# A two-block transformer step in one launch: memory products interleaved with the queries, two more norms made by halves

## The reference, cut

```python
def first_block(x, mem, ...):
    h = x
    h = h + hybrid_mixer(rmsnorm(h, mix_norm), w_in, ..., w_out_mix)
    h = h + memory_cross_attention(rmsnorm(h, xattn_norm), rmsnorm(mem, mem_norm), w_q, w_kv, w_o)
    h = h + swiglu(rmsnorm(h, ffn_norm), w_gate_up, w_down)
    return rmsnorm(h, final_norm)

def memory_cross_attention(q_in, m_in, w_q, w_kv, w_o):      # q_in 1024 x 1024, m_in 256 x 1024
    q = (q_in @ w_q).reshape(bsz, s, 4, 256)
    k, v = jnp.split(m_in @ w_kv, 2, axis=-1)                # each 256 x 1024, 4 heads of 256
    scores = jnp.einsum("bshd,bmhd->bhsm", q, k)
    probs = jax.nn.softmax(scores * (256 ** -0.5), axis=-1)
    o = jnp.einsum("bhsm,bmhd->bshd", probs, v).reshape(bsz, s, D_MODEL)
    return o @ w_o

def second_block(x, c, norm_w, ada_w, ada_b, ...):
    for layer in range(2):                                   # layer 0 even, layer 1 odd
        shift, scale, gate = jnp.split(c_act @ ada_w[layer] + ada_b[layer], 3, axis=-1)
        h = rms_norm(x, norm_w[layer]) * (1.0 + scale) + shift
        y = even_mixer(h, ...) if layer % 2 == 0 else odd_mixer(h, ...)
        x = x + gate * y
    return rms_norm(x, final_norm)
```

## Time and profile before

| | us |
|---|---|
| median of 3 executions | 3113.6 (3110.55 to 3115.39) |
| the profiled execution, its own time | 3115.71 |
| its span in the trace | 3113.9 |
| PE busy | 2950.3 (95%) |
| DVE busy | 1698.2 (55%) |
| ACT busy | 1254.4 (40%) |
| mean granted clock of TensorE | 0.975 of full |

### The profile page before, as it was taken

One profiled execution on the slowest core, in us unless ns is written; L12 is line 12 of the kernel. 1 busy time (PEld: TensorE's weight loads), 2 busy tenths in 40 slices (PEclk: granted clock), 3 DMA queues, 4 the chain that ended last, 5 costly groups with the idle time before them and its releaser, 6 DMA issues. The chain is left out here.

```text
span 3113.9 us, 38755 instructions
## 1 busy us (share of the span) xinstructions
PE 2950.3 (95%) x15570; PEld 2476.2 (80%) x15570; DVE 1698.2 (55%) x2128; ACT 1254.4 (40%) x2079; POOL 385.8 (12%) x224
## 2 busy tenths in 40 slices
PE   8999998899999999999999999889999889999997
PEld 6877886788988777888888777788888768879985
DVE  6553567654454434444444735688888634316663
ACT  5321446322443111111111335577767624427751
POOL 0000006000000000000000000355445200004410
PEclk9999999999999999999999999999999989999998
DMA  4112234022202223332231212100001321131031
GB/s 147 48 43 81 94 104 181 21 61 75 75 28 68 69 85 86 86 95 72 83 95 43 98 55 65 51 1 11 11 15 35 109 95 41 54 92 44 17 111 65
DMA packets 229280, 210.99 MB, mean 68 GB/s; under 512 B 9072, under 2 KB 202864, under 8 KB 227568
## 3 DMA queue, kind: packets, MB, share of 16 engines
q1 hardware_dynamic: 225504, 195.88, 20.6%
q10 hardware_dynamic: 3600, 12.65, 1.1%
HBM read 175.93 MB, written 30.47 MB: 66 GB/s over the span
## 5 line engine op out<-in xcount | busy, mean ns | idle before, releaser
L256 DVE TENSOR_TENSOR wl<-wf,wh 128x1024 fp32r<-128x1024 f32 (+4 forms) x239 | 251.7, 1053 | 971.8 <-ACT wh L248 971.5
L248 ACT ACTIVATE wh<-wf 128x1024 fp32r<-128x1024 f32 (+4 forms) x239 | 219.9, 921 | 1130.2 <-PE P L331 994.4
L331 PE MATMUL P<-AQ,wh 128*128 128x512 f32 x1856 | 498.8, 391 | 2.5 <-issue 2.5
L2582 POOL TENSOR_TENSOR T<-T,WST 128x1024 f32<-128x1024 f32 x128 | 242.5, 1894 | 1642.5 <-DVE WST L2554 1642.5
L331 PE MATMUL P<-XH,wh 128*128 128x512 f32 (+2 forms) x1280 | 401.0, 395 | 10.8 <-DVE XL L1334 5.2
L331 PEld LDWEIGHTS P<-AQ,wh 128*128 128x128 f32 x1856 | 348.5, 188 | 76.3 <-issue 4.1
L331 PE MATMUL P<-XL,wh 128*128 128x512 f32 (+2 forms) x1280 | 397.2, 392 | 0.0
L331 PE MATMUL P<-XH,wl 128*128 128x512 f32 (+2 forms) x1280 | 396.6, 391 | 0.0
L331 PEld LDWEIGHTS P<-XH,wh 128*128 128x128 f32 (+2 forms) x1280 | 238.8, 187 | 68.5 <-issue 16.8
L331 PE MATMUL P<-AQ,wl 128*128 128x512 f32 x928 | 286.5, 390 | 0.0
L331 PEld LDWEIGHTS P<-XH,wl 128*128 128x128 f32 (+2 forms) x1280 | 239.7, 187 | 53.3
(11 more groups left out here) (418 smaller groups left out, 5150.8 us busy)
## 6 DMA issues: line engine op xcount, KB each, us to landing
AW<-ada_w SPq DMA_DIRECT2D x48, 512.0 KB, 3.7
wf<-w_gate_up SPq DMA_DIRECT2D x44, 512.0 KB, 4.9
wf<-w_in SPq DMA_DIRECT2D x28, 512.0 KB, 3.9
scratch_h<-H SPq DMA_DIRECT2D x24, 512.0 KB, 5.7
H<-scratch_h SPq DMA_DIRECT2D x24, 512.0 KB, 7.2
scratch_g<-T ACTq DMA_DIRECT2D x22, 512.0 KB, 3.0
wf<-odd_w_in SPq DMA_DIRECT2D x20, 512.0 KB, 3.8
wf<-even_w_in SPq DMA_DIRECT2D x17, 512.0 KB, 3.9
```

Source lines behind the costliest of these rows:

```text
L248: e.activation(self.sb["wh"][i % 2][:, 0:m], self.sb["wf"][i % 2][:, 0:m], ACT.Copy).then_inc(*self.s.w_hi.up(i))
L256: e.tensor_tensor(l, f, h.bitcast(F32), ALU.subtract).then_inc(*self.s.w_lo.up(i))
L331: ins = e.matmul(self.P[slot][0:m, t:t1], w, x[:, k, t:t1], start=first and k == 0, stop=last and k == kb - 1)
L2582: e.tensor_tensor(self.px(n), self.px(n), r, ALU.mult).then_inc(*s.pool.up(("sc", n)))
```

## The change

It has four parts.

**Memory.** The slabs of the memory stage come in another order, written out in a new list MEMORY: query tiles alternate with pairs of key or value slabs. The values are made in another way (`pe_memory_values`): a slab is now 256 rows of w_kv by 512 columns, and a matmul moves 512 of these columns over 128 memory rows; four slabs add up to 512 value columns in P3, 12 matmuls each. ACT and DVE empty them in two groups: group 0 goes to a staging buffer VF first, its low part stands behind slab xv 1 2, and group 1's low part stands behind the first maximum in `dve_xattn`. Queries 0 and 1 use two T buffers. The memory's split into MM comes ahead of the stage, its reload waits only for `so`; MM and KT now lie where H lies, so that H goes to scratch in eight DMAs from ACT's queue in the `so` stage, and comes back by eight DMAs on SP's queue, four behind the last value slab, four behind the scores, ahead of the third slab of the next layer; `dve_xattn_out` waits for them. `pe_xattn` waits for queries and keys head by head, and for the values of each group.

**Norm ng.** The first half's roots stand one step later (k=4), the last two tiles' residual sums and squares are in another order, and the split of slab lq0 comes behind the first half's sum instead of behind tile 6.

**Norm n5.** eo's tile 7, the norm, the inputs x5 and the pair vo are made by halves: roots of half 0 inside k=2 of the tile's second half, its spread inside k=5; roots and spread of half 1 inside the pair.

**Norm n6.** oo's tile 7 and y are made by halves; y reads the root from P3 instead of T, in 16 DVE instructions of 512 columns, and 16 output DMAs of 256 KB follow.

```diff
+MEMORY = [("q", 0), ("q", 1), ("xk", 0), ("xk", 1), ("q", 2), ("xk", 2), ("xk", 3), ("q", 3), ("xk", 4), ("xk", 5),
+          ("q", 4), ("xv", 0, 0), ("xv", 0, 1), ("q", 5), ("xv", 0, 2), ("xv", 0, 3), ("xk", 6), ("q", 6), ("xv", 1, 0),
+          ("xv", 1, 1), ("xk", 7), ("q", 7), ("xv", 1, 2), ("xv", 1, 3)]
...
-        self.slabs("q", run(dr["w_q"], 0, 8))
-        self.slabs("xk", run(dr["w_kv"], 0, 8))
-        self.slabs("xv", run(dr["w_kv"], 1024, 8), whole=True)
+        for stage in MEMORY:
+            kind, j = stage[0:2]
+            if kind == "xv":
+                c, i = 1024 + 512 * j, stage[2]
+                self.slab(stage, cols(dr["w_kv"], c, c + 512, (2 * i, 2 * i + 2)), stage)
+            else:
...
                 e.wait_ge(*self.s.dve.to(("h1", i)))
+                e.dma_start(self.dr["hT"][:, i, :], self.H[:, i, :]).then_inc(*self.s.m[i // 4].up("out" if i % 4 == 3 else None))
...
-        e.wait_ge(*self.s.mm.to(("n2", "spread")))
-        e.wait_ge(*self.s.me.to("out"))
-        e.dma_start(self.sb["MF"][:, :], self.dr["mT"].rearrange("p k t -> p (k t)")).then_inc(*self.s.me.up("back"))
+        s = self.s
+        e.wait_ge(*s.mm.to(("so", 7)))
+        e.wait_ge(*s.me.to("out"))
+        e.dma_start(self.sb["MF"][:, :], self.dr["mT"].rearrange("p k t -> p (k t)")).then_inc(*s.me.up("back"))
+        self.sp_weights(e, self.no["wo", 0] + 2)
+        for j in range(8):
+            if j % 4 == 0:
+                e.wait_ge(*s.mm.to(("xs", 15) if j else ("xv", 1, 3)))
+            e.dma_start(self.H[:, j, :], self.dr["hT"][:, j, :]).then_inc(*s.h[j].up("memory"))
         self.sp_weights(e, self.no[("gu", 0), 0] + 2)
...
+        _, c, i = stage
+        n = self.no[stage]
+        wh, wl = self.halves(n)
+        e.wait_ge(*self.s.w_hi.to(n))
+        e.wait_ge(*self.s.w_lo.to(n))
+        if i == 0:
+            self.pe_place(e, 3)
+        for b in range(2):
+            ts = slice(128 * b, 128 * b + 128)
+            for k in range(2):
+                mh, ml = self.sb["MMH"][:, 2 * i + k, ts], self.sb["MML"][:, 2 * i + k, ts]
+                ins = self.three(e, self.P[3][:, 512 * b:512 * b + 512], mh, ml, wh[:, k, :], wl[:, k, :],
+                                 i + k == 0, (i, k) == (3, 1))
+        ins.then_inc(*self.s.mm.up(stage))
+        self.emptied[3] = [(self.s.lo, ("xv", 1)) if c else (self.s.act, ("xv", 0))]
...
+        def value(stage):
+            self.act_weights(e, self.no[stage] + 2)
+            _, c, i = stage
+            if (c, i) == (0, 3):
+                e.wait_ge(*s.mm.to(stage))
+                e.activation(sb["VF"][:, :, :], self.summed_values(), ACT.Copy).then_inc(*s.act.up(("xv", 0)))
+            elif (c, i) == (1, 2):
+                e.activation(self.values_of(sb["VMH"], 0), sb["VF"][:, :, :], ACT.Copy).then_inc(*s.hi.up(("xv", 0)))
+            elif (c, i) == (1, 3):
+                e.wait_ge(*s.mm.to(stage))
+                e.activation(self.values_of(sb["VMH"], 1), self.summed_values(), ACT.Copy).then_inc(*s.hi.up(("xv", 1)))
+        e.wait_ge(*s.me.to("back"))
+        e.wait_ge(*s.m[0].to("out"))
+        e.wait_ge(*s.lo.to(("x2", 7)))
+        for k in range(4):
+            ks = slice(2 * k, 2 * k + 2)
+            e.activation(sb["MMH"][:, ks, :], self.memory_blocks()[:, ks, :], ACT.Copy).then_inc(*s.hi.up(("m", k)))
+        between = {("q", 0): lambda e: self.act_roots(e, "n2", self.P[3][:, 0:8], 0, D, s.mm.to(("n2", "roots"))),
+                   ("q", 1): lambda e: self.act_spread(e, "n2", self.T[3])}
+        for stage in MEMORY:
+            kind, j = stage[0:2]
+            if kind == "q":
+                empty = lambda e, _, js={0: (), 1: (0, 1)}.get(j, (j,)): [query(i) for i in js]
+                self.act_tiles(e, stage, empty, stage in between and {0: between[stage]})
+            elif kind == "xk":
+                self.act_tiles(e, stage, lambda e, _, j=j: key(j))
+            else:
+                value(stage)
...
+        def query_low(j):
+            self.dve_low(e, ("q", j), self.XL[:, j, :], self.T[j == 1], self.XH[:, j, :])
+        def queries(j):
+            js = {0: (), 1: (0, 1)}.get(j, (j,))
+            for i in js:
+                query(i)
+            for i in js:
+                query_low(i)
...
+            if i == 0:
+                e.wait_ge(*s.lo.to(("q", 2 * h + 1)))
+                e.wait_ge(*s.lo.to(("xk", 2 * h + 1)))
...
+            e.wait_ge(*s.lo.to(("xv", h // 2)))
...
-        e.wait_ge(*s.lo.to(("xv", 7)))
...
+            if n == 0:
+                self.dve_low(e, ("xv", 1), self.values_of(sb["VML"], 1), self.summed_values(), self.values_of(sb["VMH"], 1))
...
+            e.wait_ge(*self.s.h[j].to("memory"))
...
-                               {3: lambda e: self.pe_half_roots(e, "ng", sb["ACC2"], 0)})
+                               {4: lambda e: self.pe_half_roots(e, "ng", sb["ACC2"], 0)})
...
-        add(0)
+        add(6)
+        e.wait_ge(*s.dve.to(("ng", "sum", 5)))
+        self.dve_square(e, "n4", 6)
+        add(7)
+        e.scalar_tensor_tensor(out=ACC2, in0=T[0], scalar=self.both_weights()[:, 6:7], in1=ACC2, op0=ALU.mult,
+                               op1=ALU.add).then_inc(*s.dve.up(("ng", "sum", 6)))
         both_sum(0)
         first_sum(0)
+        self.dve_weights(e, self.no["lq", 0])
         self.dve_half_diagonal(e, "ng", ACC2, 0, EPS * EPS)
         scaled(0, 0)
         scaled(0, 1)
-        add(1)
+        add(7, 1)
...
         self.pe_linear(e, "eo", self.AH, self.AL, lambda k: [(s.lo, ("eo", k))], lambda j: [(s.dve, ("h5", j))],
-                       paired=True)
-        self.pe_rstd(e, "n5", self.T[2], s.dve.to(("n5", "sum", 7)))
+                       paired=True, upto=7)
+        self.pe_last_by_halves(e, "eo", self.AH, self.AL, lambda j: [(s.dve, ("h5", j))], {
+            2: lambda e: self.pe_half_roots(e, "n5", self.T[2], 0),
...
+        self.dve_half_gated(e, "eo", 0, "h5", "back2", 0)
+        self.dve_half_sum(e, "n5", 0)
+        self.dve_half_diagonal(e, "n5", self.T[2], 0)
+        scaled(0, 0)
+        scaled(0, 1)
+        low(0, 0)
+        self.dve_half_gated(e, "eo", 0, "h5", "back2", 1)
+        low(0, 1)
+        self.dve_half_sum(e, "n5", 1)
+        self.dve_weights(e, self.no["eo", 7] + 2)
+        scaled(0, 2)
+        scaled(0, 3)
+        low(0, 2)
+        self.dve_half_diagonal(e, "n5", self.T[2], 1)
+        low(0, 3)
+        for k in range(4, 9):
+            if k < 8:
+                scaled(0, k)
+            if k > 4:
+                low(0, k - 1)
+        for k in range(9):
+            if k < 8:
+                scaled(1, k)
+            if k:
+                low(1, k - 1)
+    def dve_half_gated(self, e, stage, layer, name, back, h):
...
-        self.pe_linear(e, "vo", self.XH, self.XL, ready, lambda j: [(s.act, ("vo", j))], paired=True)
+        self.pe_pair_by_halves(e, "vo", "x5", lambda j: [(s.act, ("vo", j))], {
+            (0, 0, 1): lambda e: self.pe_half_roots(e, "n5", self.T[2], 1),
+            (0, 1, 3): lambda e: self.pe_half_spread(e, "n5", self.T[2], 1)})
+        self.emptied[3] = [(s.dve, ("x5", 7))]
...
+        self.dve_half_gated(e, "oo", 1, "h6", "back3", 0)
+        self.dve_half_sum(e, "n6", 0)
+        self.dve_half_diagonal(e, "n6", T[2], 0)
+        y(0, 0)
+        self.dve_half_gated(e, "oo", 1, "h6", "back3", 1)
+        y(0, 1)
+        self.dve_half_sum(e, "n6", 1)
+        for k in range(2, 5):
+            y(0, k)
+        self.dve_half_diagonal(e, "n6", T[2], 1)
+        for k in range(5, 8):
+            y(0, k)
         for k in range(8):
-            e.scalar_tensor_tensor(out=self.H[:, k, :], in0=self.H[:, k, :], scalar=self.vec("final_norm_2", k),
-                                   in1=T[3], op0=ALU.mult, op1=ALU.mult).then_inc(*s.dve.up(("y", "out", k)))
+            y(1, k)
     def sp_odd_out(self, e):
         self.sp_weights(e, len(self.order))
```

221 lines of the change are left out of this document (134 added, 87 removed).

## The result

The changed kernel takes 3070.18 us (median of 4, 3068.91 to 3076.47) against 3112.07 us of the kernel before (median of 4, 3108.58 to 3115.39). The ratio is 0.987, with a 95% interval of 0.9851 to 0.9888: 41.9 us less. The forecast was 3072.0, in a range of 3063 to 3083. The profiled execution's span is 3069.3 us, against 3113.9.

The account below looks back on a forecast made before the run. PE, busy 95% of the span, was taken as the bound. From the profiled 3115.71 us, -19.5, -2.9, -10.5 and -8.7 gave 3074.1, or 3072.0 for the median, which lay 2.1 lower; range 3063 to 3083.

Parts of the forecast that it names:

- Memory stage: Memory stage to the first maximum of the scores: 28.3 us removed, 8.4 given back, taken as -19.5 (bounds -15 and -22.5).
- the width: Memory stage's values: 96 matmuls of 512 columns at 0.2266 us instead of 384 of 128 columns, 21.1 us less.
- the waits: Memory stage: PE waits behind pairs of key or value slabs, 1.5 + 1.0 + 1.0 + 3 x 1.65 = 8.4 us given back.
- the keys: Memory stage: the keys' 192 matmuls at 0.131 us each, 25.1 in all instead of 26.33, 1.2 us less.
- the chain it named: Memory stage: ACT and DVE split the query ahead of the second slab's weights, so PE begins that slab at about 7.1 us.
- Reload and spill of H: Eight spills on ACT's queue under `so`, eight reloads on SP's: taken as hidden with 5 to 10 us to spare, cost nothing.
- rivals 1 and 2: Short memory-stage waits lower TensorE's clock: lastingly, 3128 to 3240 us, chance 2%; or briefly after each, 3082, chance 9%.
- rival 2: After each of six memory-stage waits some 1.5 us of work runs at half speed: 3082 us, chance 9%.
- Norm ng: At norm ng: roots start when PE arrives, idle 2.55 us goes, spread takes about half; -2.9 us (bounds -1.5 and -3.5).
- Norm n5: From eo's end through pair vo to ko's start: halves let work start earlier, DVE sets the pace; -10.5 us (-8 to -12.5).
- Rival 3: Norm halves bring less: half blocks cost 1.8 rather than 1.45 us, DVE waiting for ACT; 3081.5 us, chance 10%.
- Norm n6: From oo's end to the span's end: y ends 8.5 us earlier, last DMA half the size; -8.7 us (-7.5 to -9.5).

Follow-up runs that it names:

- narrow_values: Changed kernel with each 512-column value matmul made as four of 128 columns (384 matmuls instead of 96): 3081.04 us.
- late_split: Changed kernel with each query tile's high and low parts moved behind the weight split of the slab that follows: 3061.82 us.
- no_n5: Changed kernel with norm n5, its inputs and its pair made whole as before: 3080.84 us.
- before_slots: Kernel before the change, with the turn of the PSUM tiles moved on by one behind the memory stage: 3114.94 us.
- old_slots: Changed kernel with the turn of the PSUM tiles moved on by eight behind the memory stage, giving later layers their old tiles: 3072.65 us.
- no_memory: Changed kernel with the whole memory part undone (order, wide values, spills of H, two T buffers): 3088.07 us.

## Why the forecast held, and where it did not

**Memory stage.** Forecast -19.5, measured -18.0, and 18.6 by the middle of all executions. The mechanism is the forecast's: narrow_values shows the width, late_split the waits. The width came out nearly as worked out (0.2266 us a matmul, 0.112 for the narrow ones; from tile to tile 20.4 us instead of 21.1), and the keys gave 2.0 instead of 1.2.

The Trainium skill's sustained figures ("TensorE: Matmul & The Clock Gate", Back-to-back issue gap: some 131 ns at 512 columns and 81 ns at 128) are not borne out by either row of this kernel; by them the width would have brought 18.5 and not 21.

The waits were mis-sized: three of 1.4 and not 1.5, 1.0 and 1.0, three of 1.60 and not 1.65, and a seventh of 0.44 that was not in the sum: 9.4 instead of 8.4. Of the chain it named, DVE's low part is the smaller link: ACT's list held the weights. And the sum stopped at the first maximum. Behind the first scores PE waits 2.6 us for the first exponentials, since w_o's weights and the values' split stand in front of the softmax, and the attention takes 57.27 us instead of 56.33. That is the short form: in the four other executions of this stage the lower clock follows the wait and the attention takes 58.8 us, as here in no_n5 (window from its first score to w_o):

```profile
808.16:866.98 58.82, 55.45 (x450) 54.66 (x449) 48.14 (x116) 40.23 (x116) 0.00 (x0) 0.97 0.25 88
```

So this term, put at nothing, is 0.9 us in the profiled pair and up to 2.5.

**Reload and spill of H.** Costed at nothing, and so it is: the mark-to-mark time over w_o's end and the first tiles behind (896.34 to 961.6) is 65.28 us in both kernels, and no wait of PE stands in it.

**The clock (rivals 1 and 2).** Both fell for the six waits of 1.4 to 1.6 us: the clock is 1.00 over the 121.78 us, and over the same stage in the four other kernels that have it. The Trainium skill's rule of short idles that make the clock swing (same page title, A second HAM failure mode: psum-queue depth-cycling) does not show in this stage. Behind it rival 2 has a part of its truth: the wait of 2.6 us at the first scores was followed by the lower clock for 3.4 us in four executions of five, which costs some 1.5 us.

**Norm ng.** -2.9 forecast, -3.1 measured. In the profiled execution it did not come by the steps: the roots came 2.0 us earlier as said, while the spread kept its 2.08 us at the lower clock; of the gain 2.1 stood at the first scaled block, and 1.0 came in the pair behind, so the sum was right by two errors. In five of the ten executions with the new ng the steps held as well: the spread took 1.12 to 1.13 us and the first scaled block came 3.05 us earlier, as forecast.

**Norm n5.** -10.5 forecast, -10.7 measured, step by step: eo's end at 2525.88 (2525.7: the forecast's 2549.6, less the 23.9 by which the kernel is ahead at eo's start), first matmul of vo at 2526.96 (2527.3), DVE's last low part done at 2552.22 (2553.0), ko at 2556.61, with PE's last wait 1.2 us for ko0's weights (1.05). Rival 3 fell: a half block took 1.45 us (scaling at 2548.48, the next at 2549.93).

**Norm n6.** -8.7 forecast, -9.4 measured. y's last block comes 8.2 us earlier (8.5 forecast) and ends 2.6 us ahead of the span's end, not 3.8 as before; the last DMA, 256 KB, lands 2.21 us after its issue where that of 512 KB took 3.37. I had taken that for 0.2.

**Not foreseen**: the 4.35 us of the PSUM turn. It took the place of the memory's missing 1.5 and of the 1.8 that the untouched feed-forward stage was longer; the gains at n5 and n6 were 0.9 larger than said. The profiled executions lie 44.6 us apart, where 41.6 was forecast, and the medians 41.9. That the median met the forecast within 2 us is in part luck, since a term of over 4 us was missing.

## What to carry to other kernels

An engine that works down its list in order makes the list part of the schedule of everything behind it: a cheap step whose result nobody needs yet (a query's split, above all its high part, which itself waits 2.4 us for another engine) stood ahead of the weights that the matmuls needed next and cost 9.4 us of idle PE, more than the 7.4 that the interleaving brings without it. After any change in the number of tiles, look at which PSUM tile each later layer gets, above all where some layers turn over three and some over two. And where a norm stands between two layers, making it by halves pays what DVE's list allows: at n5 PE stood 13.8 of 21.1 us and 10.7 came back, with DVE busy 26.4 of 27.7 us afterwards.

## What was not expected of the hardware

The same wait of 2.52 us in the projections was followed by the lower clock in the kernel before, in before_slots and in old_slots, and by the full clock in no_memory (windows over the same part in the kernel before, old_slots and no_memory):

```profile
1768.00:1814.00 46.00, 43.48 (x189) 34.32 (x188) 24.44 (x28) 16.38 (x18) 0.00 (x0) 0.96 0.40 132
```
```profile
1749.00:1794.20 45.20, 42.68 (x187) 33.73 (x186) 23.94 (x25) 16.42 (x18) 0.00 (x0) 0.96 0.40 134
```
```profile
1761.00:1805.00 44.00, 41.48 (x187) 32.86 (x186) 24.09 (x27) 15.96 (x18) 0.00 (x0) 1.00 0.41 138
```

0.96, 0.96 and 1.00, which is 1.4 to 1.6 us of difference in the piece. The 2.6 us behind the first scores went the same way, four times with the lower clock behind it and once without, and so did the 1.27 us between ng's roots and spread. What decides it is left open. The six waits of 1.38 to 1.60 us in the memory stage never lowered it, in any of the five kernels that have them. And the first part of the feed-forward stage, whose lists are the same in all kernels, differs by up to 6 us between executions; why is left open.
